# A two-layer hybrid encoder step on one core: three split weight slots, a third PSUM pair, low parts of the weights on VectorE, and reordered loads and attention

## What is computed

```
for l in range(2):
    xn = rms_norm(x) * norm_mix_pre
    cols = xn @ w_in[l]                    # mLSTM 2056, attention 768, RWKV 1792, gates 3*1024 columns
    h_a = mlstm(cols_a)                    # 4 heads, chunks, exponential gates
    h_b = window_attention(cols_b)         # 8 query heads, 2 kv heads, chunks of 64, window 128, bias table, sinks
    h_c = rwkv(cols_c)                     # 8 heads, token shift, delta rule
    merged = sum(sigmoid(gate_i) * (h_i @ w_branch_i) for i in (a, b, c))
    x = x + rms_norm(merged @ w_out[l]) * norm_mix_post
    g, u = split(rms_norm(x) @ w_ffn_in[l])
    x = x + rms_norm((silu(g) * u) @ w_ffn_out[l])      # 2816 hidden columns
```

## Time and profile before

| | |
|---|---|
| median of 3 runs | 2640.03 us (2639.73 to 2644.22) |
| the profiled execution's own time | 2644.89 us |
| its span, first to last instruction | 2643.1 us |
| mean granted clock of PE | 0.952 |
| busy share of the span: PE, DVE, ACT, POOL | 91%, 37%, 32%, 26% |
| read from HBM | 168.62 MB, 67 GB/s with what is written |

### The profile page before, as it was taken

How to read it: one execution, slowest core, us unless ns; L and a number is a source line. 1 busy time by engine, 2 the same in 40 slices (tenths; PEclk the granted TensorE clock), 3 DMA queues, 4 the chain that set the end, 5 groups by cost and what they waited for, 6 DMA issues and landing times.

```text
span 2643.1 us, 52141 instructions
## 1 busy us (share of the span) xinstructions
PE 2404.4 (91%) x23192; PEld 2259.5 (85%) x23192; DVE 970.0 (37%) x1523; ACT 849.6 (32%) x1415; POOL 675.1 (26%) x298
## 2 busy tenths in 40 slices
PE   4998898999999899999969988999999997999998
PEld 3997788888888799999959977888888987999997
DVE  2532654554333332320053346544443324323102
ACT  3333351222341422222243334422123324222222
POOL 1321221111121233334413222211011232333442
PEclk8998999999999999999989979999998998999998
DMA  5423211111123123222234222111112131332221
GB/s 153 119 56 57 60 43 36 38 38 37 43 59 106 56 80 88 86 87 86 78 87 126 43 66 56 42 38 28 35 28 67 48 122 48 88 88 87 86 88 62
DMA packets 336073, 181.37 MB, mean 69 GB/s; under 512 B 35592, under 2 KB 332536, under 8 KB 334696
## 3 DMA queue, kind: packets, MB, share of 16 engines
q1 hardware_dynamic: 335848, 178.03, 24.1%
HBM read 168.62 MB, written 9.38 MB: 67 GB/s over the span
## 4 chain that ended last, share of the span: by engine, by line
PE 76%; DVE 8%; ACT 6%; DMA 4%; issue 3%; POOL 2%; SPq 1%; DVEq 0%; ACTq 0%; POOLq 0%
PE psum_products L577 60%; PE psum_mixer L577 15%; DMA w_raw<-in_w_in 2%; POOL w_low L2040 1%; SPq L1896 1%; ACT w_high L1093 1%; DMA w_raw<-in_w_out 1%; ACT L1093 1%; DVE x L1480 1%; ACT b_scores_even L1093 1%; DMA bias_skewed<-bias_line 0%; DVE squares_ffn L1478 0%; DVE a_dexp L1714 0%; DVE stats L1792 0%; DMA x_tokens<-in_x_sample 0%
## 5 line engine op out<-in xcount | busy, mean ns | idle before, releaser
L2040 POOL TENSOR_TENSOR w_low<-w_raw,w_high 128x1024 fp32r<-128x1024 f32 (+1 forms) x274 | 649.7, 2371 | 1851.5 <-ACT w_high L1093 1851.2
L577 PE MATMUL psum_products<-xn_high,w_high 128*128 128x272 f32 (+1 forms) x3424 | 757.4, 303 | 71.1 <-POOL w_low L2040 43.8
L577 PE MATMUL psum_products<-xn_high,w_low 128*128 128x272 f32 (+1 forms) x3424 | 724.0, 294 | 0.0
L577 PE MATMUL psum_products<-xn_low,w_high 128*128 128x272 f32 (+1 forms) x3424 | 723.1, 293 | 0.0
L577 PEld LDWEIGHTS psum_products<-xn_high,w_high 128*128 128x128 f32 x3424 | 556.9, 194 | 98.9 <-POOL w_low L2040 59.3
L577 PEld LDWEIGHTS psum_products<-xn_low,w_high 128*128 128x128 f32 x3424 | 557.9, 195 | 0.0
L577 PEld LDWEIGHTS psum_products<-xn_high,w_low 128*128 128x128 f32 x3424 | 553.8, 194 | 0.0
L1093 ACT ACTIVATE w_high<-w_raw 128x1024 fp32r<-128x1024 f32 (+1 forms) x274 | 286.7, 1047 | 273.7 <-PE psum_products L577 152.1
L577 PE MATMUL psum_products<-hidden_high,w_low 128*128 128x272 f32 x704 | 145.7, 288 | 0.0
L577 PE MATMUL psum_products<-hidden_high,w_high 128*128 128x272 f32 x704 | 145.7, 288 | 0.0
L577 PE MATMUL psum_products<-hidden_low,w_high 128*128 128x272 f32 x704 | 145.1, 288 | 0.0
(11 more groups left out here) (328 smaller groups left out, 2906.1 us busy)
## 6 DMA issues: line engine op xcount, KB each, us to landing
w_raw<-in_w_in SPq DMA_DIRECT2D x112, 512.0 KB, 3.8
w_raw<-in_w_ffn_in SPq DMA_DIRECT2D x88, 512.0 KB, 3.7
w_raw<-in_w_ffn_out SPq DMA_DIRECT2D x32, 512.0 KB, 3.4
w_raw<-in_w_out SPq DMA_DIRECT2D x16, 512.0 KB, 3.5
w_raw<-in_w_ffn_out SPq DMA_DIRECT2D x16, 384.0 KB, 3.0
x_kept<-x SPq DMA_DIRECT2D x2, 2176.0 KB, 7.8
x<-x_kept SPq DMA_DIRECT2D x2, 2176.0 KB, 8.6
w_raw<-in_w_in SPq DMA_DIRECT2D x16, 256.0 KB, 3.2
```

What stands on the lines that cost most here:

```text
L577: return pe.matmul(out, lhsT, rhs, start=start, stop=stop, skip_group_check=True)
L2040: low_ready.inc(pool.tensor_tensor(wl[:, n % NSPLIT, 0:nk], wraw[:, slot, 0:nk], wh[:, n % NSPLIT, 0:nk].bitcast(F32), ALU.subtract))
```

## The change

- NSPLIT goes from 2 to 3. Loads run NRAW (3) units ahead, not NRAW − 1; a table `ahead` says at which step which high parts are split, three units ahead.
- The low parts move from POOL to DVE (`low_part`, with a list `behind`: the part whose high half was split at a step is made before DVE's share of the next product unit or `norm_late` step). POOL keeps `c_keys`.
- `psum_products` gets six banks; banks 4 and 5 are also the mixer banks 2 and 3. `third(s)`: `cols_a` 2 and `ffn_gate` 1, the third unit of either norm, take that third pair. PE claims the two mixer banks for it, and their next claims wait until the unit is read (`also`).
- Start: the first 264 columns of the constants alone, every x tile under a semaphore of its own and transposed as it is in, layer 0's parameters issued by ACT's queue, the rest of constants and parameters later. The step `load_late` (behind `cols_a` 2 and `norm_late` 3 to 6 in layer 0) transposes layer 1's parameters and makes the bias line in mixer banks 2 and 3.
- `bias_put` and `bias_get` are steps of the plan; the store of x and the layer's small loads move from `norm_pre` to the first `norm_late`, the lora loads to `a_rows_put`. `lora` shares its place with `rstd_cols` and half of `ffn_tanh`. The constant `scan_rows` goes: one scan becomes five.
- `cols_a` 13 is no longer a filler of the mLSTM chunks but runs before them.
- Attention: `b_exps` of chunk c+1 on ACT stand inside `b_out` of chunk c, between its two copies; `b_probsT_first` and `b_probsT_second` get other places in SBUF (from `a_work` on).
- Norms: `log_table` loads the Ln table before the last square, `post_sums` puts the first sum of `norm_post` inside the last unit (behind 6 or 3 k-tiles), and the split that stood in front of `norm_post` stands behind it.

```diff
-NRAW, NSPLIT = 3, 2
+NRAW, NSPLIT = 3, 3
...
+        plan += [("bias_put", l)]
+        plan += [("load_late",)] if l == 0 else []
...
-        plan += [("cols_a", l, 8), ("a_rows_get", l)] + [("cols_a", l, j) for j in range(9, 13)]
+        plan += [("cols_a", l, 8), ("a_rows_get", l), ("bias_get", l)] + [("cols_a", l, j) for j in range(9, 14)]
...
+def third(s):
+
+    return s[0] == "cols_a" and s[2] == 2 or s[0] == "ffn_gate" and s[2] == 1
...
-        gp = ctx.enter_context(nc.psum_tensor("psum_products", [P, 4, 512], F32))
-        mp = [ctx.enter_context(nc.psum_tensor(f"psum_mixer{i}", [P, 512], F32)) for i in range(4)]
+        gp = ctx.enter_context(nc.psum_tensor("psum_products", [P, 6, 512], F32))
+        mp = [ctx.enter_context(nc.psum_tensor(f"psum_mixer{i}", [P, 512], F32)) for i in range(2)] + [gp[:, 4], gp[:, 5]]
...
+        ahead, made = {}, 3
+        for i, s in enumerate(plan):
+            if s[0] in GEMMS:
+                u = unit_no[s]
+                upto = sum(unit_no[t] <= u + (3 if s in split_no else 2) for t in split_units)
+                at_ = s
+                if plan[i + 1][0] == "norm_post":
+                    at_ = plan[i + 1]
+                if plan[i - 1][0] == "norm_pre":
+                    at_ = plan[i - 1]
+                ahead[at_] = list(range(made, max(made, upto)))
+                made = max(made, upto)
...
+                if first and ks[0] == 0:
+                    if earlier:
+                        pe.wait_ge(emptied[earlier[0]].sem, earlier[1])
+                    if pair == 2:
+                        for b in (2, 3):
+                            bank[b].claim(pe)
+                            bank[b].also = (emptied[reader].sem, turn)
...
+            def load_late():
+                pe.wait_ge(ld_prm.sem, 16 * (2 + len(PARAM_ROWS)))
+                pe.wait_ge(ld_const.sem, 16)
+                bank[2].claim(pe)
+                bank[2].filled(pe.transpose(mp[2][:, 0:NPARAM], prm_rows[0:NPARAM, 1, :], C("ident")[0:NPARAM, 0:NPARAM]), "act", "params")
+                bank[3].claim(pe)
+                bank[3].filled(mm(mp[3][0:8, 0:256], table[:], bucket[:]), "dve")
...
                 step(fn(pt0[0:min(nk, P), 0:nt * P], mp[2][0:min(nk, P), 0:nt * P], ACT.Copy), bank[2].empty["act"])
+                if c < 8:
+                    b_exps(l, c + 1)
...
+            def low_part(s):
+                n = split_no[s]
+                nk = nk_of(s)
+                dve.wait_ge(high_ready.sem, n + 1)
+                step(tt(wl[:, n % NSPLIT, 0:nk], wraw[:, unit_no[s] % NRAW, 0:nk],
+                        wh[:, n % NSPLIT, 0:nk].bitcast(F32), SUB), low_ready)
...
+                if kind in GEMMS or kind == "norm_late":
+                    for n in behind:
+                        low_part(split_units[n])
+                    behind = []
...
+                behind += ahead.get(s, ())
...
-                for s in units[0:NRAW - 1]:
+                for s in units[0:NRAW]:
                     load_unit(s)
...
-                    if kind in GEMMS and unit_no[s] + NRAW - 1 < len(units):
-                        load_unit(units[unit_no[s] + NRAW - 1])
-                    if kind == "norm_pre" and s[2] == 0:
+                    if kind in GEMMS and unit_no[s] + NRAW < len(units):
+                        load_unit(units[unit_no[s] + NRAW])
+                    if kind == "norm_late" and s[2] == 0:
...
-            low_part(units[0])
-            low_part(units[1])
             for s in plan:
-                if s[0] in GEMMS:
-                    for s2 in units[unit_no[s] + 2:unit_no[s] + 3]:
-                        if s2 in split_no:
-                            low_part(s2)
-                elif s[0] == "c_keys":
+                if s[0] == "c_keys":
```

More of the change, by code:

```diff
@@ L475, in build @@
         unit_no = {s: i for i, s in enumerate(units)}
-        split_no, unsplit_no, n_split, n_unsplit = {}, {}, 0, 0
-        for s in units:
-            if s[0] in UNSPLIT:
-                unsplit_no[s] = n_unsplit
-                n_unsplit += 1
-            else:
-                split_no[s] = n_split
-                n_split += 1
-        tiles, reads = {}, {"act": 0, "dve": 0}
-        order = []
+        split_units = [s for s in units if s[0] not in UNSPLIT]
+        split_no = {s: i for i, s in enumerate(split_units)}
+        ahead, made = {}, 3
[10 more added lines that the diff above has]
+                made = max(made, upto)
+        tiles, reads, held, turn_of = {}, {"act": 0, "dve": 0}, {}, 0
         for s in units:
@@ L491, in build @@
                 reads[r] += 1
-                tiles[key] = (len(order) % 2, r, reads[r])
-                order.append(key)
-        tile_no = {k: i for i, k in enumerate(order)}
+                pair = 2 if third(s) else turn_of % 2
+                tiles[key] = (pair, r, reads[r], held.get(pair) if pair < 2 else None)
+                held[pair] = (r, reads[r])
+                turn_of += pair < 2
         def unit_parts(s):
@@ L593, in gemm @@
                 key = s[:3] if s[0] == "ffn_out" else s
-                pair, reader, turn = tiles[key]
+                pair, reader, turn, earlier = tiles[key]
                 if s in split_no:
@@ L1936, in _ @@
-                for kv in range(2):
-                    for m in range(4):
-                        src = bass.AP(tensor=h0.tensor, offset=h0.offset + (4 * kv + m) * 64 * 256 + 63,
-                                      ap=[[255, TS], [1, KEYS_S]])
-                        put(bias_in, bias_s[TS * m:TS * m + TS, kv, :], src)
+                put(ld_prm, table[:], a["rel_bias"])
+                put(ld_prm, bucket[:], bucket_dram)
+                for name, rows in PARAM_ROWS:
+                    put(ld_prm, prm_rows[PARAM_AT[name]:PARAM_AT[name] + rows, 1, :], param_source(1, name))
```

275 lines of the change are left out of this document (154 added, 121 removed).

## The result

The changed kernel takes 2602.16 us (median of 4, 2598.07 to 2604.55), against 2640.49 of the kernel before: a ratio of 0.985, 95% interval 0.9833 to 0.9868. The direction was right, the size was not: 38 us less instead of 119, and outside the range of 2485 to 2565.

What follows compares the result with a forecast made beforehand. PE, busy 91% of the span, was taken as the bound, the gains being its idle waits. Terms 11+6+17+7+35+6+7+9+21 = 119 us off 2644.9 gave 2526, less 4.9 for the median: 2521 us, range 2485 to 2565.

Steps and rivals of the forecast that it cites:

- start: Program start: x tiles land sooner, first product at about 15.8 us instead of 26.9; gain 11 us, bounds 5 to 13.
- early part of layer 0: Layer 0's first units: the 15.76 us wait goes, a 7 us wait at load_late comes; gain 6 us, bounds 0 to 18.
- early part of layer 1: Layer 1's first units: the 16.31 us wait goes, a new one of about 2.7 comes; gain 17 us.
- mLSTM chunks: mLSTM chunks of both layers: VectorE no longer contends, 3.7 us a layer; gain 7 us, bounds 4 to 30.
- attention: Attention in both layers: waits for copied probabilities go and the clock returns to full; gain 35 us, bounds 10 to 40.
- RWKV chunks: RWKV chunks: GpSimd's waits go for 18 us, low parts in VectorE's chain cost 12; gain 6 us.
- merging and mix: Merging and mix: shorter wait on the merged input's low part, a 1.7 us weight wait goes; gain 7 us.
- norms behind sums and FFN start: Norms: rounding and table load move off, 9 us; FFN start: the 7.74 us wait and its slow clock go, 21 us.
- inside the FFN: FFN after its start: PE waits for nothing and low parts hide, 1.23 under 6.1 us; no gain counted.
- every low part counts in RWKV: Rival: all 32 low parts in RWKV's chains on the path, 39 us replacing 12, giving 2548 us; chance 0.15.
- the long wait: mLSTM chunks: the 8.39 us wait stays, since ACT waits for a weight unit issued behind three state stores.
- The clock: PE's half clock after gaps: 2.6 us regained per long gap removed, 1.7 behind shorter ones; mean clock above today's.

Runs made afterwards that it cites:

- e2: Changed kernel, but a due low part may also be made on VectorE ahead of its share of c_keys: 2574.22 us, 0.9751 of the kernel before.
- e3: Changed kernel with the low parts of the 48 gate units alone on GpSimd, the other 226 on VectorE: 2550.35 us, 0.9657 of the kernel before.
- f3: Changed kernel with the two mlstm_n state stores of each layer issued later on SP, inside attention: 2577.28 us, 0.9761 of the kernel before.
- g4: Changed kernel with the Ln table load and first sums of norm_post back in their old places, moved rounding kept: 2603.64 us, 0.9869 of the kernel before.
- f2: Changed kernel with bias_put behind cols_a 9, bias_get behind cols_a 13 and load_late behind a_rows_put: 2594.3 us, 0.9819 of the kernel before.
- e4: Changed kernel with attention's exponentials put back into b_scores of their own chunk on ACT: 2612.24 us, 0.9895 of the kernel before.
- g1: Changed kernel with the mlstm_n stores issued by ACT's queue at the first b_scores: 2570.24 us, 0.9739 of the kernel before.
- e1: Changed kernel with all 274 low parts back on GpSimd, three slots, third pair and new orders kept: 2558.46 us, 0.9695 of the kernel before.

## Why the prediction was wrong

By its own terms, with the gains from the table above (in us; the profiled spans differ by 43.8, of which the rows give 43.9):

| term | forecast | measured |
|---|---|---|
| start | 11 | 9.5 |
| early part of layer 0 | 6 | −1.6 |
| early part of layer 1 | 17 | 10.0 |
| mLSTM chunks | 7 | 13.2 |
| attention | 35 | 27.2 |
| RWKV chunks | 6 | −50.1 |
| merging and mix | 7 | 6.8 |
| norms behind sums and FFN start | 9 + 21 | 23.2 |
| inside the FFN | 0 | 5.7 |

**The step that failed is the RWKV term.** It read: "A low part of 1.23 with the 0.72 of a merging step is over it by 0.45", 16 of 32 at 0.8, 12 us. GpSimd's own waits there went as forecast, 14 us. The count was near, too: 18 low parts end a wait. But these waits sum to 51 us, 2.8 each and not 0.8, with slow clock behind the long ones. The prediction priced a low part by its duration and by how late it makes the chain of levels. That PE waits for the low part itself, and what stands ahead of it on DVE, was never asked. The order of DVE was there to read: the part of a gate unit comes behind `c_keys`, whose first operation waits for ACT. The same holds for the rival: "every low part counts in RWKV" at full price gave 39 us, and even at 2.37 us each 2585. No price per operation reaches 8.6 us for one. e2 shows this cause for 28 us; for the other 24 that e3 gives back, place and price are not told apart. 2602 less e3's 52 is inside the range given, but the forecast of 2521 lies 29 us lower still, for the terms below.

**Start.** The size held within 1.5 us. The first product ran at 17.8 and not 15.8 us: rounding waits its turn behind the scaling and the square on ACT.

**Layer 0, early.** The wait of 7 us at load_late came as forecast (7.38). The bias transfer was also foreseen, but only as a transfer in the rings. SP itself also stands at its wait from 37.3 to 60.8 us with the loads behind it: again a wait at the head of a queue, and PE's 6.50 us behind it. With a third wait, 2.96 us behind `a_rows`, the term turned negative.

**Layer 1, early.** The 16.31 went with its clock, 18.0 us. Forecast against it was 2.7 with 2.0 gained. In fact a wait of 2.8 on cols_a 16's read (4.4 with clock) and one of 4.04 behind `a_rows` (5.8 with clock) came, and 2.2 were gained: 10. Here the mechanism was right, and the new waits were mis-sized: 6.8 us without clock, for 2.7.

**mLSTM.** The reading of the long wait was right: it stayed, 6.52 us for 8.39, since the transfers behind the stores still took 12.4 us. f3 shows that this was a DMA all along, though the waits name a vector on DVE. The term is 6 us larger than forecast. In each layer 8.6 us are gained by the end of cols_a 13, which was taken out of the weave, and 3.3 of them are lost again at the next unit. I had given that move nothing. It was not tried alone.

**Attention.** The gaps went, and the slow clock in them. Of the 8 us that are missing, 3 lie at its start in layer 0: PE waits 6.40 us there, for 3.42 before, for a unit behind the second group of stores. I had written that this wait only changes its name; it grew. In layer 1 the 4.69 us cost nothing more than the waits before. The other 5 lie later in the stage; the only new wait over 1 us there is one of 1.7 a layer, and the rest was not followed up.

**Norms and FFN start.** The waits of 7.74 went whole, with the clock. The 9 for the norms was wrong. The restart of PE behind mix 7 did come 2.3 us sooner after the last product. But "at no cost" for the moved sums failed: four matmuls had run in a wait, and now stand in the last unit at 0.9 us. The first unit after it takes 1.1 us longer: 0.3 is left. g4 agrees. The Trainium skill's drain of about 1.4 us ("ScalarE: Activation LUTs", what ACT_TABLE_LOAD costs) would have made this term larger still. g4 shows no trace of it: with a load of 1.28 us back in the way, PE's restart comes 1.2 us later.

**Merging.** Right in mechanism and size: the wait on the merged input went from 4.5 to about 3.0 us, and the 1.7 is gone.

**The clock.** Its terms held: 10.3 us went with the 7.38 us wait in f2, 18.0 with the 16.31. (The prediction puts 1.7 us of slow clock behind "shorter" gaps and uses it for the longest; the traces do show 0.51 for only 3.3 us behind that one, so the number was right and the word wrong.) The mean clock was to rise; it went from 0.952 to 0.953, since new waits slowed PE as old ones had:

```profile
613.00:618.00 5.00, 4.48 (x20) 4.48 (x21) 3.96 (x6) 0.00 (x0) 0.00 (x0) 0.50 0.18 52
```

This window of the changed kernel (busy us of PE, PEld, DVE, ACT, POOL, then the granted clock) begins where the 8.64 us wait ends: PE runs at 0.50, its lower level of 1.2 GHz.

**What stays open.** What took the other 10 us of attention's waits (e4), whether the seven short waits of each layer's RWKV part are paid by place or by price, where f2 loses 7 us in layer 1, and whether g1 is faster than f3 and by queue or by time.

## What to carry to other kernels

When work moves to another engine, read that engine's program order at each place where it lands, and ask what each instruction ahead of it waits for. The cost can be the latest of these waits and many times the duration of the work; an engine that is idle for half of the time can still be the wrong queue, and a slower engine with nothing ahead in its queue the right one. The same question belongs to every wait put on a queue that also issues loads, and a wait that names a vector may end in a transfer behind a store of single elements.

## What was not expected of the hardware

Inside the FFN a gate or up unit took 6.09 us before and 6.02 after (36 units in a row, 219.1 and 216.6 us), though the list of waits shows none there in either trace. Windows of the changed kernel:

```profile
930.00:1290.00 360.00, 360.00 (x2876) 360.00 (x2875) 153.88 (x172) 100.74 (x120) 0.00 (x0) 1.00 0.31 89
```

That is 125.2 ns a matmul, for 127 before, but the matmuls did not become faster: within a unit they start every 125 ns in both kernels. The difference sits where an up unit begins. In the kernel before, GpSimd's low part and PE's first matmul of such a unit:

```profile
1020.93 2.39 POOL L2040 TENSOR_TENSOR w_low<-w_raw,w_high 128x1024 fp32r<-128x1024 f32 x1 [4.53 <-ACT w_high L1093]
...
1023.37 0.39 PE L577 MATMUL psum_products<-xn_high,w_high 128*128 128x272 f32 x1
```

The low part ends at 1023.32 and PE starts 0.05 us later, and so it is with 20 of the 22 up units of each layer: each was held by its low part for a time too short to be listed. "Inside the FFN PE waits for nothing" was not quite true. A unit takes 6.02 in e1 as well, with low parts on GpSimd, and no more without the third pair; three slots, with splitting three units ahead, are what these share. The 72 units are 5.0 of the 5.7 us of the table.

A low part on DVE takes 1.23 us alone and took 2.17 while GpSimd ran a multiplication of `c_keys` beside it for 1.1 us (610.68 to 612.38 above): the sharing that slowed DVE before slows it also when DVE's own operation is the low part.
